# Row stages in wide steps, a last MLP chunk in an order of its own, and rows kept without the norm's weight and shift

## The chip, the cores and the metric

One core of a Trainium2 chip runs the whole program in one launch. The metric is the device time in microseconds (us); the kernel before has a median of 2984.6 us over 3 runs (2983.01 to 2986.8). Instructions run on five engines that wait for each other by semaphores: TensorE (PE, with its weight loads PEld), VectorE (DVE), ScalarE (ACT), GpSimd (POOL) and SyncE (SP), whose queue issues nearly all DMAs.

## The reference

Two transformer layers over 1024 image tokens and 256 context tokens of width 1024. Layer 0 mixes tokens by windowed attention with a sink beside a gated spatial mixing, layer 1 by neighbourhood attention on a 16 x 64 grid. What matters here is what stands around the mixers and in the MLP:

```python
def _layer_norm(x, g, b):
    mu = jnp.mean(xf, axis=-1, keepdims=True)
    var = jnp.mean(jnp.square(xf - mu), axis=-1, keepdims=True)
    y = (xf - mu) * lax.rsqrt(var + LN_EPS)
    return (y * g + b).astype(x.dtype)

def _squared_relu_mlp(h, w1, w2):
    return jnp.square(jax.nn.relu(h @ w1)) @ w2
```

In each layer the mixer reads h = x * (1 + scale_a) + shift_a and x becomes norm(ALPHA * x + gate_a * mixer(h)) with ln1's weight and shift; the MLP reads h = x * (1 + scale_m) + shift_m and x becomes norm(ALPHA * x + gate_m * mlp(h)) with ln2's. ALPHA is the square root of 2, and scales, shifts and gates are rows of 1024 numbers computed from the conditioning vectors, one set for the image tokens and one for the context tokens. Layer 1 gives image tokens only.

## The kernel before

Tokens lie in tiles of 128 rows: 10 in layer 0 (8 of the image, 2 of the context), 8 in layer 1. Every matrix product is done in three: both operands are split into a rounded high part and the low rest (`hth`/`htl` for the transposed activations, `wah`/`wal`, `wbh`/`wbl` for weights), and high x high, low x high and high x low are added in PSUM. The program is a row of eight stages with a barrier at the end of each:

- `stage_modulation` computes the first scales and shifts from 8 x 1 MB of weights; behind them SP fetches three tiles of x.
- `stage_rows(0, 0)`: each tile is transposed by TensorE (8 blocks of 128x128), modulated by ScalarE in 8 instructions of 128x128 (`modulate`, L388), then rounded and subtracted by VectorE (`split_ht`, L440 and L443) into `hth` and `htl`. The input has three buffers, so SP fetches tile t + 3 when tile t is transposed.
- `stage_window` (layer 0's attention, and the inputs of the mixing), and `stage_mix`: rows come from DRAM, are normalised (ScalarE L1287), mixed (PE L1349), completed (VectorE L1329, L1334), transposed, copied to `bot` (ScalarE L1293, `leave`; two buffers) and stored to `cat_dram` (SP L1279). SP issues the eight loads of the projection's weights `raww` (L1276) ahead of the first store.
- `stage_block(layer)`: first the projection, tile by tile: products, times the gate (L2147), plus ALPHA x (L2151, from `xres`, one buffer), moments, normalisation without weight and shift (L2163), transposes (L2267), modulation into `hth`. ln1's weight and shift are folded into the scale and shift columns (`fold`), so h is right without them; GpSimd applies them to the rows (L2057, L2059), and SP stores these in `x_dram` (L1912). ScalarE waits for the last store (`s_b`, `s_store`) before the MLP's first relu, because the MLP's buffers lie over those of the projection. In layer 1 the stored rows are fetched into `k.y` and multiplied by ALPHA (`begin_y`, L2111), and the MLP's sums are added there.
- The MLP runs in 16 chunks of 256 hidden columns. A step c does, for each group of 512 tokens, the second products of chunk c - 1 (`second`, L2305 to L2307) and then the first products of chunk c (L2329 to L2331), whose result passes ScalarE (relu L2032, square L2034), GpSimd (square in full precision L2078) and VectorE (the low part L2227). `sum_tile` (L2173) adds a tile's products into `y`. Steps are an instruction loop (`over_steps`); in layer 1 the last step is written out (`ending`), in layer 0 it is not: after the loop the second products of chunk 15 follow for all tiles, then per tile the gate (GpSimd L2085), ALPHA x and the moments (VectorE `residual`, L2180 to L2186), with x fetched into two buffers.
- `stage_rows(0, 2)`: between the layers: ln2 is applied by VectorE in two instructions a tile with rows of weight and shift (L475, L478), the result goes to `x_dram` and is transposed, modulated in 8 pieces, copied into grid order by ScalarE (`placed`, L395) and split by VectorE (L443).
- `stage_attention` (layer 1), and `stage_block(1)`, which ends in the output.

Every stage after the first clears the semaphores of the stage before; VectorE does it ahead of its first instruction (`clear_last`). Each engine carries out its instructions in the written order. `C` is 6, the number of VectorE counts a projection tile, and `nth(c, t)` numbers the second products.

## Time and profile before

| | |
|---|---|
| median of 3 runs | 2984.6 us (2983.01 to 2986.8) |
| profiled execution, its own time | 2985.59 us |
| its span | 2983.8 us, granted clock 0.967 |
| TensorE busy | 2799.8 us, 94% |
| VectorE busy | 1361.5 us, 46% |
| ScalarE busy | 912.1 us, 31% |
| GpSimd busy | 533.6 us, 18% |
| DMA | 238.95 MB, mean 80 GB/s |

The profile page cuts the span into 40 slices and gives each engine's busy share in tenths; the lines PEclk (granted TensorE clock) and DMA are on the same scale:

```profile
PE   6999995999999999999957999999799999999998
DVE  3575454563333333333383555555555333333336
PEclk7999997999999999999978999999999999999999
DMA  6574225441011010010042111110256111111112
```

A matmul's busy time overlaps the next one's, so a full PE slice tells that TensorE had work, not how fast it went. The dips of PE lie at the start, around slice 7 (460 to 510 us), around slices 21 and 22 (1500 to 1590) and around slice 29 (2150 to 2190).

### The profile page before, as it was taken

The page shows a single profiled execution, that of the slowest core. Times are in us where ns is not written, and L with a number is a line of the kernel's source. Part 1 is how long each engine was busy: PE and PEld are TensorE (multiplying, and loading weights), DVE is VectorE, ACT ScalarE, POOL GpSimd, SP SyncE. Part 2 cuts the span into 40 slices and gives each one's busy share as a digit, 9 for nine tenths or more (in the row PEclk, how much of TensorE's full clock was granted, in tenths as well). Part 3 has the DMA queues.
Part 4 walks back from the last instruction along what each step waited for, and adds up shares of the span by engine and source line. Part 5 has one row for each costly group of instructions (what it writes and reads, how often), then busy time and mean ns, then how long its engine had stood idle before and what let it go on. Part 6 is the DMA issues. An engine that isn't in the chain of part 4 may idle for free. (4 is left out here: it accounts for less than half of the span.)

```text
span 2983.8 us, 40578 instructions
## 1 busy us (share of the span) xinstructions
PE 2799.8 (94%) x15614; PEld 2296.1 (77%) x15614; DVE 1361.5 (46%) x2159; ACT 912.1 (31%) x1704; POOL 533.6 (18%) x365
## 2 busy tenths in 40 slices
PE   6999995999999999999957999999799999999998
PEld 3666774788888888888846888888677888888886
DVE  3575454563333333333383555555555333333336
ACT  4244553341121121111224344443433212211222
POOL 0000000341121121121140000000034223323321
PEclk7999997999999999999978999999999999999999
DMA  6574225441011010010042111110256111111112
GB/s 251 184 307 157 70 67 186 147 136 43 28 48 36 28 56 28 28 56 28 30 146 83 36 36 51 36 36 8 85 141 191 48 45 48 56 42 42 56 42 57
DMA packets 192673, 238.95 MB, mean 80 GB/s; under 512 B 15992, under 2 KB 153840, under 8 KB 186416
## 3 DMA queue, kind: packets, MB, share of 16 engines
q1 hardware_dynamic: 192272, 237.30, 24.8%
q8 instruction: 76, 1.25, 0.2%
q14 instruction: 37, 0.30, 0.0%
q10 hardware_dynamic: 288, 0.10, 0.0%
HBM read 203.72 MB, written 37.88 MB: 81 GB/s over the span
## 5 line engine op out<-in xcount | busy, mean ns | idle before, releaser
L2173 DVE TENSOR_TENSOR y<-y,pair 128x1024 f32<-128x1024 f32 x280 | 341.5, 1220 | 334.9 <-PE pair L2307 334.9
L2305 PE MATMUL pair<-m_wbh,m_ath 128*128 128x512 f32 x1120 | 437.1, 390 | 4.2 <-DVE y L2173 2.9
L2307 PE MATMUL pair<-m_wbh,m_atl 128*128 128x512 f32 x1120 | 437.9, 391 | 0.0
L2306 PE MATMUL pair<-m_wbl,m_ath 128*128 128x512 f32 x1120 | 436.9, 390 | 0.0
L2227 DVE TENSOR_TENSOR m_atl<-m_sq,m_ath 128x512 fp32r<-128x512 f32 x156 | 100.8, 648 | 646.2 <-POOL m_sq L2078 646.2
L2032 ACT ACTIVATE m_rel<-pair 128x512 f32<-128x512 f32 x160 | 88.9, 555 | 983.6 <-PE pair L2331 973.1
L2078 POOL TENSOR_TENSOR m_sq<-m_rel 128x512 f32<-128x512 f32 x160 | 155.2, 970 | 1125.6 <-ACT m_rel L2032 1125.5
L2331 PE MATMUL pair<-hth,m0n_wal 128*128 128x512 f32 (+1 forms) x768 | 272.2, 354 | 0.0
L2330 PE MATMUL pair<-htl,m0n_wah 128*128 128x512 f32 (+1 forms) x768 | 272.1, 354 | 0.0
L2329 PE MATMUL pair<-hth,m0n_wah 128*128 128x512 f32 (+1 forms) x768 | 271.5, 354 | 0.0
L2305 PEld LDWEIGHTS pair<-m_wbh,m_ath 128*128 128x128 f32 x1120 | 210.3, 188 | 50.3 <-DVE y L2173 4.6
L2307 PEld LDWEIGHTS pair<-m_wbh,m_atl 128*128 128x128 f32 x1120 | 210.2, 188 | 44.8
L2306 PEld LDWEIGHTS pair<-m_wbl,m_ath 128*128 128x128 f32 x1120 | 210.2, 188 | 44.5
L2329 PE MATMUL pair<-hth,m1n_wah 128*128 128x512 f32 x512 | 200.5, 392 | 3.4 <-DVE htl L2100 3.4
L2331 PE MATMUL pair<-hth,m1n_wal 128*128 128x512 f32 x512 | 200.8, 392 | 0.0
L2330 PE MATMUL pair<-htl,m1n_wah 128*128 128x512 f32 x512 | 200.7, 392 | 0.0
L2330 PEld LDWEIGHTS pair<-htl,m0n_wah 128*128 128x128 f32 x768 | 145.1, 189 | 21.6
L2329 PEld LDWEIGHTS pair<-hth,m0n_wah 128*128 128x128 f32 x768 | 145.1, 189 | 21.1
L2331 PEld LDWEIGHTS pair<-hth,m0n_wal 128*128 128x128 f32 x768 | 145.1, 189 | 20.1
L1611 DVE CUSTOM_DVE_ANT_0 a_sx<-pair,a_tab 128x640 f32<-128x640 f32 (+1 forms) x128 | 96.0, 787 | 86.8 <-PE pair L1703 86.8
L2025 ACT ACTIVATE m_wbh<-m_rawb 128x1024 fp32r<-128x1024 f32 x62 | 62.3, 1053 | 198.9 <-PE pair L2307 198.9
L2282 PE MATMUL pair<-r_wh,r_cath 128*128 128x512 f32 x288 | 116.5, 404 | 6.4 <-DVE r_catl L2095 5.9
(270 smaller groups left out, 5239.8 us busy)
## 6 DMA issues: line engine op xcount, KB each, us to landing
a_ring<-in_w_mod SPq DMA_DIRECT2D x40, 1024.0 KB, 9.1
m_rawb<-in_mlp_w SPq DMA_DIRECT2D x64, 512.0 KB, 4.4
m_rawa<-in_mlp_w SPq DMA_DIRECT2D x60, 512.0 KB, 4.1
x_rows<-r_res SPq DMA_DIRECT2D x28, 512.0 KB, 5.0
r_raw<-cat_cols SPq DMA_DIRECT2D x18, 512.0 KB, 6.3
mod_w<-in_w_mod SPq DMA_DIRECT2D x8, 1024.0 KB, 12.3
r_xin<-in_x SPq DMA_DIRECT2D x16, 512.0 KB, 4.3
gate_pre<-a0g_gout SPq DMA_DIRECT2D x20, 256.0 KB, 2.0
```

Of the source, the lines that this page charges most:

```text
L1611: dve.tensor_tensor_reduce(sx[:, n % 2, hh, 0:keys], two[:, at:at + keys], table(hh, t), -1.0, 3.0e38, ALU.add, ALU.min, sm[:, 0:1]).then_ ...
L2032: act.activation(rel[:, m % 2, 0:n], k.bank[4 + jj % NB1][:, 0:n], ACT.Relu).then_inc(s_relu, 1)
L2078: pool.tensor_tensor(sq[:, m % 2, 0:n], r, r, ALU.mult).then_inc(s_sq, 1)
L2173: dve.tensor_tensor(k.y[:, t, :], k.y[:, t, :], k.pair[t % 2][:, :], ALU.add).then_inc(s_y, 1)
L2227: dve.tensor_tensor(atl[:, m, a:a + n], sq[:, m % 2, 0:n], f32(ath[:, m, a:a + n]), ALU.subtract).then_inc(s_atl, 1)
L2282: pe.matmul(o, cath[:, t % 2, kt, :], wh[:, kt, n], start=kt == 0, stop=False)
L2305: pe.matmul(o, ath[:, m, ts], bh[:, m, cols], start=m == 0, stop=False)
L2306: pe.matmul(o, ath[:, m, ts], bl[:, m, cols], start=False, stop=False)
L2307: i = pe.matmul(o, atl[:, m, ts], bh[:, m, cols], start=False, stop=m == M - 1)
L2329: pe.matmul(o, wah[:, m, kt, :], xh, start=kt == 0, stop=False)
L2330: pe.matmul(o, wah[:, m, kt, :], xl, start=False, stop=False)
L2331: i = pe.matmul(o, wal[:, m, kt, :], xh, start=False, stop=kt == KT - 1)
```

## The change

All of these at once:

- **First rows stage** (`stage_first`): all ten tiles of x are fetched behind the modulation's weights. TensorE transposes four tiles before a group's first step is whole; a step is one block row of 128 features x 512 tokens (256 for the context). ScalarE modulates it in one instruction, and the rounding is VectorE's in even steps and ScalarE's in odd ones.
- **Mixing**: `bot` has six buffers, and each store is followed by one of the loads of `raww`.
- **Layer 0's last MLP chunk** has a step of its own, with the second products of chunk 15 begun before the first products end. x and the gate rows are fetched into the space of `hth`/`htl` (x in four buffers). GpSimd gates and VectorE adds and takes moments in an order written out by hand (`ending_first`).
- **Between the layers** (`stage_between`): wide steps as in the first stage. VectorE normalises in one instruction a tile, without weight and shift; ln2's are folded into layer 1's scale and shift columns; the eight image tiles are stored without them.
- **Layer 1's projection** reads these rows into two buffers, and GpSimd applies ln2's weight and shift to them before VectorE adds them. Its own rows are stored without ln1's weight and shift; `begin_y` applies these, in two instructions a tile where there was one. Only one gate row is fetched.
- **Clears** of semaphores are GpSimd's in each stage.

The core of the diff:

```diff
-            dve.sem_clear(s)
+            pool.sem_clear(s)
 # stage_modulation
-            for t in range(3):
-                sp.dma_start(x_ahead[:, t, :], io["x"][0][t * P:(t + 1) * P, :]).then_inc(s_ahead[t], 16)
+            for t in range(XT + CT):
+                sp.dma_start(x_ahead[:, t, :], x).then_inc(s_ahead[t], 16)
 # stage_first (stage_between alike, with placed() around hth and htl)
+            for i, (a, n, kt) in enumerate(steps):
+                act.wait_ge(s_tr, i + 1)
+                if i >= NB:
+                    act.wait_ge(s_hl, i - NB + 1)
+                act.activation(modt[:, i % NB, 0:n], k.bank[kt][:, 0:n], ACT.Identity, scale=col(SC_A), bias=col(SH_A)).then_inc(s_mod, 1)
+                if by_act(i):
+                    high(i)
...
+                if by_act(i):
+                    dve.wait_ge(s_ha, i // 2 + 1)
+                else:
+                    dve.tensor_copy(hi, v).then_inc(s_hd, 1)
+                    dve.wait_ge(s_hd, i // 2 + 1)
+                dve.tensor_tensor(k.htl[:, kt, a:a + n], v, f32(hi), ALU.subtract).then_inc(s_hl, 1)
 # stage_between, VectorE
+            def normalise(t):
+                dve.tensor_scalar(res[:, t, :], y[:, t, :], k.mv[:, t, 0:1], rstd[:, 1, t:t + 1], ALU.subtract, ALU.mult).then_inc(s_norm, 1)
 # stage_mix
-            for u in range(KT):
-                sp.dma_start(raww[:, u, :], io["ab_w_out"][0][u * P:(u + 1) * P, :]).then_inc(s_raww[u], 16)
+    NT = 6
+                if t < KT:
+                    sp.dma_start(raww[:, t, :], io["ab_w_out"][0][t * P:(t + 1) * P, :]).then_inc(s_raww[t], 16)
 # stage_block, layer 0, last chunk, TensorE
+                    if ends(c) and not final:
+                        if g == 0:
+                            second(c - 1, 1)
+                            second(c, 0)
+                        elif g == 1:
+                            second(c - 1, 2)
+                            second(c, 1, range(4, 7))
+                        else:
+                            second(c, 1, range(7, 8))
+                            second(c, 2)
 # the same, VectorE (ending_first)
+                for t in range(4):
+                    sum_tile(c, t)
+                    if t >= 2:
+                        residual(t - 2)
+                low(1, 0)
+                residual(2)
+                low(1, 1)
+                residual(3)
+                for t in range(8, tiles):
+                    sum_tile(c - 1, t)
+                for t in range(4, 7):
+                    sum_tile(c, t)
+                    if t == 6:
+                        residual(4)
+                for m in range(M):
+                    low(2, m)
+                residual(5)
+                for t in range(7, tiles):
+                    sum_tile(c, t)
+                    residual(t - 1)
+                residual(tiles - 1)
 # stage_block, layer 1, GpSimd
+            for t in range(tiles) if final else ():
+                pool.wait_ge(s_xr[t % 2], 16 * (t // 2 + 1))
+                x = xres[:, t % 2, :]
+                pool.tensor_tensor(x, x, lng[:, :], ALU.mult).then_inc(s_past, 1)
+                pool.wait_ge(s_past, 2 * t + 1)
+                pool.tensor_tensor(x, x, lnb[:, :], ALU.add).then_inc(s_past, 1)
 # begin_y, layer 1
-                        dve.tensor_scalar(k.y[:, t, :], k.y[:, t, :], ALPHA, None, ALU.mult).then_inc(s_y, 1)
+                        dve.scalar_tensor_tensor(out=y, in0=y, scalar=ALPHA, in1=ln1[0], op0=ALU.mult, op1=ALU.mult).then_inc(s_past, 1)
+                        dve.wait_ge(s_past, 2 * tiles + t + 1)
+                        dve.scalar_tensor_tensor(out=y, in0=ln1[1], scalar=ALPHA, in1=y, op0=ALU.mult, op1=ALU.add).then_inc(s_y, 1)
```

## Rows read from the trace of the kernel before

**Rows 1.** Windows by seam: start:end, length, busy us by engine, PEclk, DMA share, GB/s.
```profile
29.50:61.60 32.10, 18.05 (x80) 15.03 (x80) 19.18 (x20) 28.01 (x80) 0.00 (x0) 0.55 0.45 148
461.50:506.70 45.20, 21.73 (x129) 19.54 (x129) 17.87 (x37) 13.67 (x22) 0.00 (x0) 0.69 0.77 268
1492.30:1537.10 44.80, 28.55 (x120) 21.84 (x118) 38.57 (x51) 0.80 (x2) 31.83 (x11) 0.89 0.34 112
1537.10:1589.40 52.30, 19.68 (x80) 15.70 (x80) 37.91 (x39) 39.59 (x99) 0.00 (x0) 0.50 0.44 151
2147.50:2185.00 37.50, 27.68 (x102) 21.40 (x103) 18.55 (x23) 12.75 (x13) 0.00 (x0) 0.86 0.82 243
2262.00:2292.00 30.00, 23.78 (x95) 18.64 (x95) 18.59 (x19) 10.95 (x20) 15.19 (x8) 0.89 0.91 245
```

**Rows 2.** Timeline, first rows stage: start, us, instruction [idle before, releaser].
```profile
29.61 3.40 PE L530 MATMUL pair<-kept_ident,r_xin 128*128 128x128 f32 x16 [0.62 <-PEq L141]
...
34.52 0.69 DVE L440 CAST hth<-r_modt 128x1024 fp32r<-128x1024 f32 x1 [5.23 <-ACT r_modt L388]
```

**Rows 3.** Groups by line, first rows stage: busy us, mean ns, idle before.
```profile
L388 ACT ACTIVATE r_modt<-pair,kept_mod 128x128 f32<-128x128 f32 x80 | 28.0, 708 | 28.6 <-PE pair L530 28.6
```

**Rows 4.** DMA view of 0 to 62 us: GB/s in 40 slices.
```profile
GB/s 0 48 111 399 420 433 423 423 424 419 423 428 428 428 423 415 412 410 79 39 264 309 369 396 315 0 277 106 277 66 293 85 254 0 0 11 0 0 0 0
```

**Rows 5.** Page, costliest groups: busy us, mean ns, idle before.
```profile
L2227 DVE TENSOR_TENSOR m_atl<-m_sq,m_ath 128x512 fp32r<-128x512 f32 x156 | 100.8, 648 | 646.2 <-POOL m_sq L2078 646.2
```

**Rows 6.** Timeline of the mixing stage.
```profile
466.93 0.22 DVE L1308 RECIPROCAL gate_rstd<-gate_rstd 128x10 f32<-128x10 f32 x1 [10.87 <-issue]
...
472.52 0.76 DVE L1329 TENSOR_TENSOR gate_bo<-pair,gate_plus 128x256 f32<-128x256 f32 x2 [1.58 <-PE pair L1349]
...
489.64 0.60 ACT L1293 ACTIVATE gate_bot<-pair 128x512 f32<-128x512 f32 x1 [12.30 <-DMA cat_cols<-gate_bot]
```

**Rows 7.** Groups by line, 1495 to 1537 us, the end of layer 0's MLP.
```profile
L2183 DVE BATCH_NORM_STATS2 m_stats<-y 128x6 f32<-128x512 f32 x20 | 12.9, 685 | 0.3
L2180 DVE SCALAR_TENSOR_TENSOR y<-m_rawa,y 128x1024 f32<-128x1024 f32 x10 | 12.7, 1272 | 0.0
L2173 DVE TENSOR_TENSOR y<-y,pair 128x1024 f32<-128x1024 f32 x10 | 11.9, 1188 | 4.2 <-PE pair L2307 4.2
```

**Rows 8.** Timeline of GpSimd and TensorE there.
```profile
1496.43 2.40 POOL L2085 TENSOR_TENSOR y<-y,m_rawb 128x1024 f32<-128x1024 f32 x1 [3.06 <-DVE y L2173]
...
1501.81 3.32 POOL L2085 TENSOR_TENSOR y<-y,m_rawb 128x1024 f32<-128x1024 f32 x1 [0.30 <-DVE y L2173]
...
1509.36 0.50 PE L2305 MATMUL pair<-m_wbh,m_ath 128*128 128x512 f32 x1 [0.68 <-DVE y L2173]
```

**Rows 9.** Timeline, rows stage between the layers.
```profile
1543.43 0.21 DVE L454 RECIPROCAL r_rstd<-r_rstd 128x10 f32<-128x10 f32 x1 [6.54 <-DMA r_lnb<-in_ln_b]
...
1551.28 1.15 ACT L395 ACTIVATE hth<-r_modt 128x512 fp32r<-128x512 f32 x2
```

**Rows 10.** Instructions on the tile r_res: ns least/median/most, first and last start.
```profile
L2151 DVE SCALAR_TENSOR_TENSOR r_res<-r_xin,r_res x18: 1225/1904/2224, 533.5 to 2261.0; 128x1024 f32<-128x1024 f32 x18
L2163 DVE TENSOR_SCALAR r_res<-r_res,r_mv,r_rstd x18: 811/814/815, 536.9 to 2265.6; 128x1024 f32<-128x1024 f32 x18
```

**Rows 11.** Timeline, layer 1's projection and the MLP's first chunk.
```profile
2177.31 0.17 DVE L2125 COPY r_lnc<-pair 128x16 f32<-128x16 f32 x1 [10.14 <-DMA r_gate<-gate_rows]
...
2183.53 1.97 PE L2267 MATMUL pair<-kept_ident,r_res 128*128 128x128 f32 x8 [5.62 <-DVE r_res L2163]
...
2185.68 2.39 POOL L2057 TENSOR_TENSOR r_res<-r_res,r_lng 128x1024 f32<-128x1024 f32 x1 [88.51 <-PE pair L2267]
...
2276.49 0.79 PE L2329 MATMUL pair<-hth,m1n_wah 128*128 128x512 f32 x1 [3.43 <-DVE htl L2100]
...
2277.68 0.60 ACT L2032 ACTIVATE m_rel<-pair 128x512 f32<-128x512 f32 x1 [6.07 <-DMA x_rows<-r_res]
...
2291.49 0.49 PE L2305 MATMUL pair<-m_wbh,m_ath 128*128 128x512 f32 x1 [1.24 <-DVE y L2111]
```

657 lines of the change are left out of this document (281 added, 376 removed).

## The prediction

> **What bounds the kernel now.** I first cut the span by stages (busy time in windows). In the matmul stages TensorE is busy for all but a few per cent of the window and its granted clock is near 1.00; what is slower is six seams, and the change touches all of them: the first rows stage, the mixing stage, the end of layer 0's MLP, the rows stage between the layers, and the two ends of layer 1's projection [rows 1]. In these TensorE is busy for 18 of 32, 22 of 45, 29 of 45, 20 of 52, 28 of 38 and 24 of 30 us. So I read the timeline of each engine in those windows alone and asked there which wait ends last. The matmuls of the long stretches keep their number and shapes, so I give them no change.
>
> **First rows stage, 32.1 us now.** ScalarE sets it: 80 modulations of 128x128 take 28.0 us, 0.35 each [rows 3]. They become 24, sixteen of 128x512 and eight of 128x256, plus 12 rounding copies that alternate with VectorE. A 128x512 read of PSUM costs ScalarE 0.60 [rows 6], a 128x512 copy 0.58 (half of 1.15) [rows 9]; instructions that follow each other without a wait overlap by about 0.1. A pair of wide steps is 0.50 + 0.60 + 0.55 = 1.65, eight pairs 13.2; the four pairs of half size at 1.1 are 4.4. ScalarE's sum is 17.6. VectorE has per pair one cast (0.69 for 1024 columns, so about 0.4 for 512 [rows 2]) and two subtractions of 0.65 [rows 5]: 1.7, the same speed. What is new is the wait ahead of it: the first step needs the 25th of 32 transposes (0.21 each, from 16 in 3.40 [rows 2]), so it starts at 29.6 + 5.3 = 34.9, not at 31.6. The loads cover that: 8.4 MB of weights and then tiles of 0.52 MB stream at some 420 GB/s (each figure of the row is 1.55 us of the window) [rows 4], so tiles 0 to 2, in already, are followed by tile 3 at about 29.5 and tile 9 at 37. End: 34.9 + 17.6 + 1.5 for the last chain and the barrier = 54.0 at best; VectorE and ScalarE wait for each other through four buffers, so I take 55, against 61.6: **-6.5** (ends -9, if the loads and the overlap are perfect, and 0).
>
> **Mixing stage, 45.2 us now.** Two waits. VectorE starts at 466.93, having cleared the old semaphores since 461.6; without them it starts when the square root is done, some 3.5 earlier [rows 6]. Second, ScalarE's third copy out waits 12.30 for a store that is queued behind the eight loads of the projection's weights (4.2 MB) [rows 6]. With six output buffers and one load per store this wait goes. What is late next: the products begin at about 470 instead of 472.5 [rows 6], and a pair of tiles costs VectorE 2.9 (0.76 for two halves and 0.69, twice) plus the turn through TensorE and ScalarE, 3.5 to 4.5, so the fifth pair is out by 488 to 491. Then the queue: the 5.2 MB of gate rows end at about 477, and 4.2 MB of weights and 2.6 MB of stores remain; at 400 GB/s they need 17 us, that is until 494.5, and the last store is behind them. End 495, against 506.7: **-11.5** (-15 if arithmetic sets the end, -7 at the stage's mean of 268 GB/s [rows 1], which would give 500 to 502). The next stage starts no earlier by the clears alone: its first low part waits for the load of the columns anyway. Nothing there.
>
> **End of layer 0's MLP, 44.8 us now.** After the last first product, ten tiles pass through VectorE one by one (sum 1.19, residual 1.27, two moments of 0.69, aggregate 0.2: about 3.8 a tile), and TensorE waits some 0.7 for it in each [rows 7, 8]; TensorE alone needs 2.73 for the twelve products of a tile (3.8 less the wait and less the slower start after it). The change moves the products of four tiles ahead of the second first-product and three ahead of the third. I laid VectorE's written order against TensorE's, counting from P, the start of the last chunk's first four tiles (1470.2 now, 22.15 before 1492.3). GpSimd's gating takes 2.4 alone, 3.3 when VectorE runs beside it [rows 8]; I use 3.3. Gating of tiles 0 to 3 ends P+17.1 and holds the square of the second group by 0.1 only. Tile 8 of the chunk before is summed at P+28.1, and TensorE, ready at 27.6, waits 0.5. TensorE ends at P+50.2. VectorE is late: sum of tile 8 at 51.3, residual 7 at 54.0, sum 9 at 55.2, its gating at 58.5, last residual P+61.2 = 1531.4 against 1536.9: **-5.5** (-9 with gating at 2.4 and no slip, 0 if VectorE's two extra waits for squares, at most 2.7 each, each fall late).
>
> **Rows stage between, 52.3 us now.** VectorE first waits 6.54, for clears and the norm's rows [rows 9]; then ten tiles in 46 us, in lockstep with ScalarE's eight small modulations. After: square root and reciprocal until +0.65; two normalisations at 0.81 [rows 10], four small folds of 0.2, two more normalisations: the fourth tile is ready at +4.6, its transpose and the first wide modulation at +5.5. From there VectorE: eight pairs of a cast and two subtractions, 0.45 + 0.65 + 0.65 and 0.1 of gaps (14.8), four half pairs of 1.1 (4.4), six normalisations in between (4.7): 23.9. ScalarE has 18.5 beside it and is covered. End +29.4, with the barrier 30, against 52.3: **-22** (-25 to -18). The cast writes runs of eight columns; no row has it, so I bound it by half the contiguous one, 0.35, and the subtraction's 0.65; eight of them move the sum by 2.4 at most, and I take 0.45. The Trainium skill bears on this (VectorE: DVE Perf Modes, What auto-detection actually checks): a single-source operation inside SBUF takes the double rate where the outermost dimensions are equal, which it would here; that puts the cast near the low end. The trace agrees for the contiguous one, 0.69 for 1024 columns [rows 2]; no row shows the strided. By the rule the sum would be 0.8 better, by the other end 1.6 worse.
>
> **Layer 1's projection, this one costs.** First end. VectorE now begins when the second gate row lands, 2177.3, and the residual row lands at 2179.3; tile 0 is normalised and TensorE's transposes, 5.62 late, run at 2183.53 [rows 11]. One gate row fewer puts the first residual row in its place, 2177.3. But GpSimd must then multiply and add on it: 2 x 2.4 and gaps, 4.9 [rows 11], so VectorE gets it at 2182.2, 2.9 later than now, and beside GpSimd on the second tile its 1.22 becomes 1.9 (least and median) [rows 10]: **+3.6** (0 to +5). In the middle the row's path is load 5 + GpSimd 4.9 + VectorE 1.9 = 12, and with two buffers it has the time of two tiles. From tile 0's transposes at 2183.5 to the wait at 2276.5 [rows 11] eight tiles pass, over 11 each, so 22: covered.
> Other end. The last row's weight and shift, 4.8 on GpSimd ahead of the last store, go. ScalarE's first relu waits for that store now [rows 11]. So the relu moves from 2277.7 to 2275, the last low part of h from 2276.5 to 2274.9 (TensorE waits 3.43 for it now [rows 11]), and the last five rows of y are fetched 5 earlier. But y then needs two operations of 1.22 a tile where one of 0.69 did, and TensorE's first product on y waits for seven tiles, its second for all eight. VectorE is free for tiles 1 to 7 at about 2281; 7 x 2.5 = 17.5, so 2295.9 for the seventh, against 2291.49 now [rows 11]: +4.5. TensorE then stands for some 7 us instead of 1.24. After the stall of 3.43 its two jobs took 13.8 instead of 10.9, so a restart at a low clock costs 2 to 3; one moves from 2276 to 2296. I count nothing more for it. Other end **+4.5** (0 to +9). Both are ahead of a stretch in which TensorE is never short of work, so nothing gives them back.
>
> **Clears on GpSimd** elsewhere: in the window and attention stages TensorE's first matmuls wait for its own ten warm-up matmuls, and GpSimd's tables are wanted tens of us later. Nothing. Instructions of the last chunk, now written out once more, run as in layer 1: nothing.
>
> **Sum.** -6.5 - 11.5 - 5.5 - 22 + 3.6 + 4.5 = -37.4. The profiled execution took 2985.6 (span 2983.8 and 1.8 around it); it lies 1.0 above the median of 2984.6, so 2947 to 2948. I say 2948. The own range of this case is 2938 to 2957.
>
> **Rivals.**
> 1. The seams are bound by something else soon. For it: in the mixing stage a queue of 6.8 MB, in the MLP's end VectorE's written order, where one late square shifts all behind it; in layer 1, two stands and two cold restarts. Against: each length above is a sum of rows. With the weak ends, 0, -7, 0, -18, +5, +9: -11, with half of these slips -24: 2962, band 2957 to 2978. Chance 0.20.
> 2. Layer 1's additions are hidden: the residual row lands so early that GpSimd is done when the gate is, and y is ready in time, since loads come 5 earlier. For it: VectorE is idle through much of that stretch. Against: its order puts y behind the low parts of the chunk. The sum without them: 2940, and with better ends in the other seams 2932. Chance 0.13.
> 3. Slower: TensorE's clock. The last chunk of layer 0 now has a hand-over between VectorE and TensorE at each of some 20 products, and the clock could fall in them. A restart costs 2.9 (13.8 against 10.9, above); from 14 of them the gains are gone, and with 16 it is 2994. Against: now TensorE stops 0.7 at each of ten tiles in the MLP's end, and only the first product after a stop is longer, 0.50 [rows 8]. Chance 0.03.
> 4. The parts don't add: GpSimd's clears stand in the way of its work on the first rows, or something unseen. Near 2982, chance 0.02.
>
> **How the numbers follow.** The forecast has 0.62. The range takes in rival 2's middle and rival 1's nearer half: 2936 to 2962. A difference of 0.2% is 6 us, about what can be told from none: under 2979 is faster. That holds for the forecast, rival 2 and nearly all of rival 1: 0.95; same 0.02, slower 0.03.
>
> **What would show it.** First rows stage: 24 modulations and an end near 55. Mixing: no idle over 2 us ahead of the copy out, and a stage of some 34. MLP's end: VectorE's last residual about 11 after TensorE's last product. Between: 30 long, VectorE nearly full. Layer 1: GpSimd's two operations between the landing and the first residual, and seven y tiles in a row ahead of the first product on y. I am wrong if the between stage is over 35, or if the delay on y is absent.

## The result, and the profile after

| | before | after |
|---|---|---|
| median, runs of the same session | 2985.7 us (4 runs, 2983.01 to 2987.27) | 2969.0 us (4 runs, 2967.44 to 2971.22) |
| ratio | | 0.9946 (95% interval 0.9928 to 0.9963) |
| profiled execution, its own time | 2985.6 us | 2971.2 us |
| its span, granted clock | 2983.8 us, 0.967 | 2969.4 us, 0.973 |

The kernel is faster by 16.7 us, and 37 were forecast: the sign is right, the size is not, and 2969.0 lies outside the range of 2936 to 2962. The windows of the seams show where, start:end in us, length, busy us by engine, then PEclk, DMA share and GB/s. They answer to those of before [rows 1] in the same order; the third starts with the last chunk and not with its end, and the last two are a little longer than their counterparts.

```profile
30.02:56.62 26.60, 14.41 (x80) 11.06 (x79) 18.23 (x36) 21.18 (x37) 0.04 (x1) 0.76 0.44 149
...
455.00:492.31 37.31, 19.79 (x129) 17.73 (x130) 18.12 (x37) 13.61 (x23) 0.00 (x0) 0.73 0.92 325
...
1456.00:1519.80 63.80, 50.49 (x241) 41.34 (x239) 45.94 (x57) 4.08 (x8) 31.41 (x14) 0.96 0.19 56
1519.80:1551.05 31.25, 14.90 (x81) 13.38 (x82) 25.73 (x51) 21.69 (x38) 0.04 (x1) 0.72 0.52 186
...
2109.70:2152.00 42.30, 27.04 (x96) 20.28 (x96) 19.52 (x23) 12.66 (x13) 10.18 (x4) 0.78 0.68 209
...
2230.00:2300.00 70.00, 49.01 (x199) 38.83 (x198) 45.45 (x35) 15.08 (x26) 23.72 (x12) 0.85 0.55 158
```

To compare kernels I cut every trace at the same instructions: TensorE's first warm-up matmul behind each rows stage and at the start of layer 1's projection, VectorE's last copy of layer 0's attention, ScalarE's first copy of the projection's weights, the end of VectorE's last aggregate of layer 0 (`moments`), TensorE's transposes of layer 1's first tile. Lengths in us:

| stretch | before | after | change | forecast |
|---|---|---|---|---|
| start to the end of the first rows stage | 61.9 | 56.6 | -5.3 | -6.5 |
| layer 0's window attention | 393.7 | 394.0 | +0.3 | 0 |
| mixing | 51.1 | 41.7 | -9.4 | -11.5 |
| layer 0's projection and MLP | 1030.2 | 1027.5 | -2.7 | -5.5 |
| between the layers | 52.6 | 31.3 | -21.3 | -22 |
| layer 1's attention | 558.1 | 558.7 | +0.6 | 0 |
| layer 1's projection, up to the first transposes | 35.9 | 42.2 | +6.3 | +3.6 |
| from there to the end | 800.3 | 817.4 | +17.1 | +4.5 |
| span | 2983.8 | 2969.4 | -14.4 | -37.4 |

Layer 0 gave 38.5 of the 45.5 forecast. The loss is in layer 1: 24.1 where 8.1 were priced, and 12.6 of the difference lies in the last stretch. Its timeline there (start in us, duration in us, instruction, and in brackets the idle time before it and what ended it), first VectorE:

```profile
2252.79 2.07 DVE L2039 SCALAR_TENSOR_TENSOR y<-y,r_over 128x1024 f32<-128x1024 f32 x1
2254.89 1.22 DVE L2041 SCALAR_TENSOR_TENSOR y<-r_over,y 128x1024 f32<-128x1024 f32 x1
...
2266.45 3.37 DVE L2039 SCALAR_TENSOR_TENSOR y<-y,r_over 128x1024 f32<-128x1024 f32 x1
2269.85 3.25 DVE L2041 SCALAR_TENSOR_TENSOR y<-r_over,y 128x1024 f32<-128x1024 f32 x1
2273.02 3.39 DVE L2039 SCALAR_TENSOR_TENSOR y<-y,r_over 128x1024 f32<-128x1024 f32 x1
2276.44 3.28 DVE L2041 SCALAR_TENSOR_TENSOR y<-r_over,y 128x1024 f32<-128x1024 f32 x1
```

GpSimd's in the same us, the low parts of the first weight and the gating of the second:

```profile
2265.69 6.33 POOL L1987 TENSOR_TENSOR m1n_wal<-m_rawa,m1n_wah 128x1024 fp32r<-128x1024 f32 x2 [6.28 <-ACT m1n_wah L1923]
2271.98 6.66 POOL L1993 TENSOR_TENSOR m_rawb<-m_rawb,y 128x1024 f32<-128x1024 f32 x2
```

And what TensorE and ScalarE do about it:

```profile
2273.33 0.79 PE L2273 MATMUL pair<-m_wbh,m_ath 128*128 128x512 f32 x1 [15.88 <-DVE y L2041]
2273.91 0.63 PE L2274 MATMUL pair<-m_wbl,m_ath 128*128 128x512 f32 x1
```
```profile
2246.53 0.60 ACT L1947 ACTIVATE m_rel<-pair 128x512 f32<-128x512 f32 x1 [6.56 <-DMA x_rows<-r_res]
```

The seven tiles of y were priced at 7 x 2.5 = 17.5. They take from 2252.79 to 2279.7, 26.9, and the last four operations take 3.25 to 3.39 each, not 1.22. That is not a slower VectorE: GpSimd's pairs of operations take 6.33 and 6.66 in those us. In layer 0 such a pair, beside VectorE's sums of y, leaves both engines at their own times:

```profile
1095.54 4.76 POOL L1987 TENSOR_TENSOR m0n_wal<-m_rawa,m0n_wah 128x1024 fp32r<-128x1024 f32 x2 [0.87 <-ACT m0n_wah L1923]
```
```profile
1096.36 1.22 DVE L2106 TENSOR_TENSOR y<-y,pair 128x1024 f32<-128x1024 f32 x1 [1.23 <-PE pair L2275]
```

The difference is where the inputs lie: those of the sum are `y` and `pair`, which is in PSUM, while both inputs of the operations that begin y are in SBUF. With both there, each engine stands while the other runs. (By the Trainium skill, SBUF — State Buffer, "SBUF: two separate sides", the port pair that GpSimd and VectorE share is "an exclusive lock, not a bandwidth split", and a VectorE operation with two SBUF inputs takes it against a GpSimd operation that reads SBUF; these rows agree.)

TensorE has finished the first products by 2257.4 and stands 15.88. The relu, forecast 2.7 earlier than its old place, is where it was: the kernel is 31.5 ahead at the transposes (2183.53 against 2151.99), and 2246.53 + 31.5 is 2278.1, against 2277.68 [rows 11]. The last store still lands only at 2246.4. It is issued at 2234.82 and takes 11.6 us to land; in the kernel before it was issued at 2272.63 and landed at 2277.50, after 4.9.

The first end of the projection, VectorE and then GpSimd:

```profile
2138.68 0.17 DVE L2055 COPY r_lnc<-pair 128x16 f32<-128x16 f32 x1 [8.39 <-DMA r_gate<-gate_rows]
...
2145.72 3.27 DVE L2084 SCALAR_TENSOR_TENSOR r_res<-r_xin,r_res 128x1024 f32<-128x1024 f32 x1 [5.16 <-POOL r_xin L1974]
```
```profile
2140.86 2.34 POOL L1972 TENSOR_TENSOR r_xin<-r_xin,r_lng 128x1024 f32<-128x1024 f32 x1 [81.54 <-DMA r_xin<-x_rows]
2143.28 2.34 POOL L1974 TENSOR_TENSOR r_xin<-r_xin,r_lnb 128x1024 f32<-128x1024 f32 x1
2145.58 2.34 POOL L1972 TENSOR_TENSOR r_xin<-r_xin,r_lng 128x1024 f32<-128x1024 f32 x1
```

VectorE's addition is released at 2145.72, 0.14 behind the start of GpSimd's multiplication of the second tile, and lasts 3.27: until that one is done (2147.92), and then 1.07, nearly its own 1.2.

### The profile page after: what moved, and what is told of

It reads as the page before. It is cut to its first block and busy times, and to the rows that moved or that the text cites. A ratio compares the mean times of both kernels' runs of the same rounds, so it can differ in the third digit from the quotient of the medians.

```text
span 2969.4 us, 40552 instructions
## 1 busy us (share of the span) xinstructions
PE 2793.5 (94%) x15615; PEld 2289.2 (77%) x15615; DVE 1367.4 (46%) x2195; ACT 887.6 (30%) x1598; POOL 533.5 (18%) x365
## 3 DMA queue, kind: packets, MB, share of 16 engines
q8 instruction: 78, 1.28, 0.2%
## 5 line engine op out<-in xcount | busy, mean ns | idle before, releaser
L2273 PE MATMUL pair<-m_wbh,m_ath 128*128 128x512 f32 x1080 | 422.1, 391 | 16.8 <-DVE y L2041 16.8
L2275 PE MATMUL pair<-m_wbh,m_atl 128*128 128x512 f32 x1080 | 423.2, 392 | 0.0
L2274 PE MATMUL pair<-m_wbl,m_ath 128*128 128x512 f32 x1080 | 422.2, 391 | 0.0
L2273 PEld LDWEIGHTS pair<-m_wbh,m_ath 128*128 128x128 f32 x1080 | 203.4, 188 | 60.7 <-issue 16.3
L2275 PEld LDWEIGHTS pair<-m_wbh,m_atl 128*128 128x128 f32 x1080 | 203.3, 188 | 43.3
L2274 PEld LDWEIGHTS pair<-m_wbl,m_ath 128*128 128x128 f32 x1080 | 203.3, 188 | 43.2
L2296 PEld LDWEIGHTS pair<-htl,m0n_wah 128*128 128x128 f32 x768 | 145.1, 189 | 21.6
## 6 DMA issues: line engine op xcount, KB each, us to landing
mod_w<-in_w_mod SPq DMA_DIRECT2D x8, 1024.0 KB, 12.2
```

Of the source, the lines that this page charges most:

```text
L2273: pe.matmul(o, ath[:, m, ts], bh[:, m, cols], start=m == 0, stop=False)
L2274: pe.matmul(o, ath[:, m, ts], bl[:, m, cols], start=False, stop=False)
L2275: i = pe.matmul(o, atl[:, m, ts], bh[:, m, cols], start=False, stop=m == M - 1)
L2296: pe.matmul(o, wah[:, m, kt, :], xl, start=False, stop=False)
```

## The experiments

Differences of a whole run are given against the changed kernel's 2969.0, from medians; each ratio is to the kernel before, measured on the same chip, whose median moved between 2984.3 and 2986.2 from one chip or session to the next. Differences of 2 us in the whole are therefore not told from none, and there I read the stretches above. They come from the profiled execution, and the changed kernel's took 2971.2, 2.2 above its median: a stretch can show up to 2 us more than the medians do. The diffs are cut to the lines that matter; the semaphores that go with them are left out.

**1. GpSimd waits for y.**

```diff
+                if final and not starts(c):
+                    pool.wait_ge(s_y, tiles)
```

> GpSimd's weight work for the second chunk (the low part of w1, the gate on w2) waits until all eight y tiles are begun. Theory A (VectorE's two-input operations on y and GpSimd's two-input operations block each other): the four y operations that took 3.3 to 3.4 us fall to 1.2, y is complete some 8 us earlier after the relu, and the whole is 7 to 9 us faster than the changed kernel (near 2961). Theory B (the y operations are slow because the fetches of w1 and w2 run then): they stay at 3.3, no change. Theory C (GpSimd's work is itself due at that time): TensorE waits for the low part of w1 instead, and what is gained is given back, within 2 us of the changed kernel.

Measured: 2964.9 us, ratio 0.9929 (0.9913 to 0.9946), 4.1 less; the last stretch is 811.5, 5.9 less. Groups by line over 2100 to 2340 us (busy us, mean ns, idle before):

```profile
L2041 DVE SCALAR_TENSOR_TENSOR y<-y,r_over 128x1024 f32<-128x1024 f32 x8 | 12.1, 1512 | 5.0 <-DMA y<-x_rows 5.0
...
L2043 DVE SCALAR_TENSOR_TENSOR y<-r_over,y 128x1024 f32<-128x1024 f32 x8 | 9.8, 1225 | 0.3
```

The second operation is back at 1.225 us in all eight tiles (a mean of 1.734 in the changed kernel), though the fetches of the weights run on: theory B is out. Tiles 1 to 7 take 18.5 us and not 26.9. TensorE's waits for y fall only from 16.8 to 12.2, because its first product on y waits for the sixth of these seven tiles, 3.8 us earlier in the stretch than in the changed kernel, and the seventh is then done before it is wanted. So the blocking is real. What this run takes away of it is worth 5.9 in the last stretch, less than half of what the end lost; two first operations of 2.06 and 2.07 beside GpSimd's squares stay. The whole gains less than theory A's 7 to 9 and more than theory C's 2, and what C names isn't seen: up to 2340 us TensorE waits for nothing of GpSimd's.

**2. One operation for y.**

```diff
-                        dve.scalar_tensor_tensor(out=y, in0=y, scalar=ALPHA, in1=ln1[0], op0=ALU.mult, op1=ALU.mult).then_inc(s_past, 1)
...
-                        dve.scalar_tensor_tensor(out=y, in0=ln1[1], scalar=ALPHA, in1=y, op0=ALU.mult, op1=ALU.add).then_inc(s_y, 1)
+                        dve.tensor_scalar(y, y, ALPHA, None, ALU.mult).then_inc(s_y, 1)
```

> begin_y in layer 1 is one multiplication by ALPHA again; ln1's weight and shift are left out of the residual. Theory A (the second operation and the block with GpSimd are the price of this seam): the first second product comes within 1 us of where the kernel before has it, counted from the end of the projection, so 15 to 17 us faster than the changed kernel (near 2953). Theory B (the store of the last rows sets it, as it did before): the gain is at most 3 us.

Measured: 2955.4 us, ratio 0.9896 (0.9879 to 0.9912), 13.6 less. TensorE's and VectorE's groups over 2100 to 2300 us:

```profile
L2271 PE MATMUL pair<-m_wbh,m_ath 128*128 128x512 f32 x32 | 13.2, 412 | 3.8 <-DVE y L2039 3.8
```
```profile
L2039 DVE TENSOR_SCALAR y<-y 128x1024 f32<-128x1024 f32 x8 | 5.7, 747 | 9.8 <-DMA y<-x_rows 9.8
```

TensorE's wait is 3.8 and no longer 16.8, and the last stretch is 802.6: 14.8 of its 17.1 are back. The medians show a little less than theory A's 15 to 17, and theory B's 3 is out. What this end lost is, but for 2.3 us, y's two operations with what blocks them; this run takes out both at once and doesn't divide them.

**3. Residual rows without GpSimd.**

```diff
-                pool.tensor_tensor(x, x, lng[:, :], ALU.mult).then_inc(s_past, 1)
...
-                pool.tensor_tensor(x, x, lnb[:, :], ALU.add).then_inc(s_past, 1)
```

> GpSimd's multiplication and addition on layer 1's residual rows are left out (ln2's weight and shift are missing in that residual). Theory A (GpSimd's two operations stand in front of tile 0's residual, and with it its next one blocks VectorE): tile 0's residual starts when its row has landed, and transposes of tile 0 come 6 to 7 us earlier, all of which is kept: near 2962.5. Theory B (the row's landing sets it): at most 2 us.

Measured: 2964.0 us, ratio 0.9928 (0.9911 to 0.9944), 5.1 less; the stretch up to the first transposes is 7.6 shorter, and those begin at 2143.87:

```profile
2139.65 1.23 DVE L2080 SCALAR_TENSOR_TENSOR r_res<-r_xin,r_res 128x1024 f32<-128x1024 f32 x1 [0.29 <-DMA r_xin<-x_rows]
```

The row is then ready when the gate is, and the addition takes 1.23. GpSimd's two operations cost 7.6 here, which is theory A; the spans of the profiled executions differ by 7.6 as well, the medians by 5.1. The last stretch is as long as in the changed kernel (817.9 against 817.4): the two ends are separate.

**4. Clears on VectorE.**

```diff
-            k.clear_last(pool)
+            k.clear_last(dve)
```

> Only the clearing of the old semaphores goes back from GpSimd to VectorE, in every stage. Theory A (a clear costs about 0.1 us and counts where VectorE is first in line): mixing stage 2 to 3.5 us longer, rows stage between 5 to 6.5 longer, nothing in the other stages: 7 to 10 us slower than the changed kernel (near 2977.5). Theory B (clears are hidden by loads and tables): under 2 us.

Measured: 2976.0 us, ratio 0.9965 (0.9952 to 0.9977), 7.0 more. The two places where VectorE cleared, in the mixing and between the layers:

```profile
460.00 0.22 DVE L1059 RECIPROCAL gate_rstd<-gate_rstd 128x10 f32<-128x10 f32 x1 [10.85 <-issue]
```
```profile
1524.85 0.22 DVE L1190 RECIPROCAL r_rstd<-r_rstd 128x10 f32<-128x10 f32 x1 [6.95 <-issue]
```

Between the layers the wait is 6.95 where the changed kernel has 0.64, and block and clears together are 6.8 longer. In the mixing VectorE starts 3.7 later (10.85 behind its last copy, 7.15 in the changed kernel), and the stage is 41.2 us against 41.7: no longer at all. So theory A holds between the layers and fails in the mixing, where the clears were worth nothing, and the total of 7.0 is all from the one place.

**5. The last store ahead of y.**

```diff
-                    for i in range(2):
-                        sp.wait_ge(s_store[i], 16 * len(range(i, 3, 2)))
-                    for u in range(3):
-                        sp.dma_start(k.y[:, u, :], rows(k.x_dram, u, True)).then_inc(s_yx[u], 16)
                 for u in ([t - 1] if 0 < t < tiles - 1 else [t - 1, t] if t else []):
...
+                for i in range(2):
+                    sp.wait_ge(s_store[i], 16 * len(range(i, 3, 2)))
+                for u in range(3):
+                    sp.dma_start(k.y[:, u, :], rows(k.x_dram, u, True)).then_inc(s_yx[u], 16)
```

> SP fetches the first three rows of y behind the last stores of layer 1's projection, no longer ahead of them; nothing else is changed. Theory A (the last store, issued at 2234.12 and landed at 2246.4, waits in the queue behind loads that nothing ahead of the MLP's second step needs): the first relu of layer 1's MLP starts some 3 to 6 us earlier than its 2246.5, but VectorE's rows of y, which set the end, start no earlier than the low parts of h allow, so the time falls by 1 to 5: 2964 to 2968. Rival B (the store is slow by itself, or bound by the loads of the weights ahead of it): the relu moves by under 1.5 and the time stays at 2969 within 2. Rival C (y's first row lands later and VectorE then waits for it): slower, 2970 to 2974.

Measured: 2973.0 us, ratio 0.9959 (0.9945 to 0.9973), 4.0 more (3.2 in the last stretch): rival C. The store is indeed faster: issued at 2232.51, it lands at 2239.19, after 6.7 us and not 11.6. Groups of TensorE and of ScalarE over 2100 to 2310 us:

```profile
L2295 PE MATMUL pair<-hth,m1n_wah 128*128 128x512 f32 x48 | 19.8, 412 | 6.0 <-DVE htl L2025 6.0
```
```profile
L1947 ACT ACTIVATE m_rel<-pair 128x512 f32<-128x512 f32 x6 | 3.6, 595 | 50.0 <-PE pair L2297 42.5 <-DVE htl L2025 7.4
```

The relu no longer waits for the store but for the last low part of h, and this for y's first row, which lands at 2241.42 and which VectorE's order puts ahead of it. TensorE waits 6.0 for the low part (3.3 in the changed kernel). Two late waits lie side by side; mending one shows the other.

**6. The gate row behind the first residual row.**

```diff
+            if final:
+                residual_in(0)
             for c in range(3 - XB):
-                sp.dma_start(rgate[:, c, :], gate_row).then_inc(s_row, 16)
-            for t in range(XB):
+                sp.dma_start(rgate[:, c, :], gate_row).then_inc(s_rg if final else s_row, 16)
+            for t in range(1 if final else 0, XB):
                 residual_in(t)
...
-            pool.wait_ge(s_row, 48 if final else 64)
+            pool.wait_ge(s_row, 32 if final else 64)
```

> At layer 1's first end the loads go in the order weight row, shift row, residual row 0, gate row, residual row 1, and GpSimd waits only for the first three. Theory A (tile 0 is late because GpSimd's multiplication and addition start only when the gate row has landed): GpSimd starts some 2 us earlier, TensorE's transposes of tile 0 are 2 to 3 earlier (2149 to 2150 instead of 2152), and the time is 2966 to 2968. Rival B (VectorE's addition, 3.27 while GpSimd works on the second tile, and not the loads, is what is late): GpSimd starts earlier but VectorE, which waits for the gate, meets GpSimd at another place; the transposes move by under 1 and the time is 2969 within 1.5.

(In the diff the DMA's address is shortened to `gate_row`.) Measured: 2965.9 us, ratio 0.9937 (0.9921 to 0.9954), 3.1 less; the transposes come 2.3 earlier in their stretch, and GpSimd starts at 2135.99, 2.4 earlier in it: theory A. VectorE's timeline:

```profile
2138.46 0.17 DVE L2062 TENSOR_TENSOR kept_mod<-kept_mod,r_lnt 128x16 f32<-128x16 f32 x1
2138.55 2.32 DVE L2063 TENSOR_TENSOR kept_mod<-kept_mod,r_lnc 128x16 f32<-128x16 f32 x1
2140.79 1.28 DVE L2082 TENSOR_TENSOR r_res<-pair,r_gate 128x512 f32<-128x512 f32 x2
2142.10 2.12 DVE L2089 SCALAR_TENSOR_TENSOR r_res<-r_xin,r_res 128x1024 f32<-128x1024 f32 x1
```

An operation of 16 columns takes 2.32 instead of 0.17, because GpSimd began 2.38 us of work at 2138.46. In this the blocking is seen at its barest: its price is what is left of the other engine's instruction, whatever the size of one's own. Rival B is thus seen too, but it takes back only 0.1 of the 2.4.

**7. Mixing: three weight loads ahead of the first store.**

```diff
+            for u in range(3):
+                sp.dma_start(raww[:, u, :], io["ab_w_out"][0][u * P:(u + 1) * P, :]).then_inc(s_raww[u], 16)
...
-                if t < KT:
+                if t + 3 < KT:
```

> In the mixing stage three of the eight loads of the projection's weights are issued ahead of the first store, the other five behind stores 0 to 4, instead of eight behind eight stores. Theory A (the stage ends 7 us after its last store is issued because that store queues behind 4.2 MB of loads issued just before it): the loads get done earlier while the queue is slack, the stage ends 2 to 4 us earlier than its 492.3, and the time is 2965 to 2967. Rival B (the queue is full from the stage's start, by the gate rows of 5.2 MB, so order doesn't matter): stage and time stay within 1.5 of 492.3 and 2969. Rival C (ScalarE waits for stores again): the copies out wait over 3 us and the time is over 2970.

Measured: 2971.1 us, ratio 0.9953 (0.9937 to 0.9970), 2.1 more; the stage is 41.8 us (41.7 in the changed kernel). That is rival B's stage, and theory A is out; the time lies 0.6 above B's bound, which the differences between sessions cover. ScalarE does wait for stores again, as rival C has it, but for 1.53, 1.28 and 1.40 us and not over 3, and the stage doesn't show it. The mixing of the changed kernel, 450 to 493 us in 40 slices:

```profile
GB/s 0 204 71 40 44 8 0 192 345 250 345 341 373 356 398 410 406 391 381 387 373 400 392 389 374 415 367 408 372 393 394 389 399 380 402 379 333 101 14 0
```

From about 458.6 to 490 us the queue carries 333 to 415 GB/s, but for one slice (each is 1.08 us), 12.5 MB in the whole window. From the stage's first issue at 456.57 on, the stage is the time of its transfers: weights loaded earlier or an earlier start of VectorE (experiment 4) don't shorten it. Two things stay untried: weights loaded behind the last store, and transfers in the 6 us before that first issue, in which the queue is nearly idle (0 to 71 GB/s from the third slice on).

**8. y interleaved with the sums.**

```diff
+        if final:
+            body(1)
...
                         for t in tiles_of(g):
                             sum_tile(c - 1, t)
+                            if final and isinstance(c, int) and c == 1 and g == 0:
+                                begin_y(t + 4, t + 5)
...
-                            begin_y(1, tiles)
+                            begin_y(1, 4)
```

> Layer 1's y: VectorE begins only tiles 0 to 3 ahead of the second step, and tiles 4 to 7 one by one between the sums of tiles 0 to 3, so TensorE's first product on y waits for three tiles' operations and not for seven. The same operations, the same sum of work. Theory A (the lost 12 us of this end are a wait of TensorE for seven tiles in a row, of which 9.4 are GpSimd's and VectorE's blocking of each other): TensorE's idle time ahead of its first product on y falls from 16.8 to 5 to 8 us, later waits of 1 to 2 come in its place, and the time is 2957 to 2962. Rival B (VectorE has no slack in the second step, so what is moved comes back as waits between the products): the time is over 2965. Rival C (GpSimd's two low parts of the weights, delayed by VectorE, take the place of the wait): TensorE's wait stays above 12 and the time is over 2964.

Measured: 2952.8 us, ratio 0.9889 (0.9873 to 0.9906), 16.2 less, more than theory A gave. TensorE's groups over 2100 to 2310 us:

```profile
L2307 PE MATMUL pair<-hth,m1n_wah 128*128 128x512 f32 x64 | 26.3, 412 | 4.4 <-DVE htl L2029 4.4
L2285 PE MATMUL pair<-m_wbh,m_ath 128*128 128x512 f32 x41 | 16.2, 395 | 0.7 <-DVE y L2116 0.7
```

The wait of 16.8 is 0.7, and B and C are out. The last stretch is 801.0, and it was 800.3 before the change. The work is the same and the blocking is still there, as the next rows show, but it costs TensorE nothing, because four of the tiles are wanted later:

```profile
2268.30 2.29 DVE L2043 SCALAR_TENSOR_TENSOR y<-y,r_over 128x1024 f32<-128x1024 f32 x1
2270.63 3.31 DVE L2048 SCALAR_TENSOR_TENSOR y<-r_over,y 128x1024 f32<-128x1024 f32 x1
```

**9. The same, and y's tile 0 behind the last low part of h** (the diff is against experiment 8).

```diff
-            begin_y(0, 1 if final else XT)
             split_ht(tiles - 1)
+            if final:
+                begin_y(0, 1)
```

> The interleaved y of the run before, and VectorE begins y's tile 0 behind the last low part of h, no longer ahead of it. Theory A (the last low part waits for y's first row to land, and TensorE for the low part): TensorE's wait at the last first-product of tile 7, 4.4 us in the interleaved run and 3.3 in the changed kernel, falls under 1, its next first-products run at the high clock, and the time falls by 2 to 6 against 2952.8: 2947 to 2951. Rival B (the relu, which waits for the last store until 2247, holds the squares and so TensorE's second products): TensorE's wait only moves to the second products, the time stays within 1.5 of 2952.8. Rival C (VectorE is at the low parts too early and blocks with GpSimd's rows of the second weight): over 2954.

Measured: 2953.3 us, ratio 0.9898 (0.9881 to 0.9914), 0.5 from experiment 8: rival B. TensorE's groups over 2100 to 2340 us:

```profile
L2310 PE MATMUL pair<-hth,m1n_wah 128*128 128x512 f32 x87 | 34.1, 391 | 1.2 <-DVE htl L2029 1.2
L2288 PE MATMUL pair<-m_wbh,m_ath 128*128 128x512 f32 x64 | 26.1, 408 | 5.3 <-DVE y L2119 4.4 <-DVE m_wbl L2171 0.8
```

The wait for the low part falls from 4.4 to 1.2, and 4.6 more come back at the second products, most of it as a wait for VectorE's first sum, which stands behind its row of y.

**10. Gating of 64 columns in layer 0's last chunk.**

```diff
-                pool.tensor_tensor(y, y, end_gate[cond(t)], ALU.mult).then_inc(s_gated, 1)
+                pool.tensor_tensor(k.y[:, t, 0:64], k.y[:, t, 0:64], end_gate[cond(t)][:, 0, 0:64], ALU.mult).then_inc(s_gated, 1)
```

> GpSimd's gating in layer 0's last chunk covers 64 of 1024 columns (the rest of the gate is left out). Theory A (the end of layer 0's MLP is 2.6 later than laid out since GpSimd's 2.4 to 3.3 us a tile stand in VectorE's way, 2.2 of it in one sum): the last sum and residual fall by 4 to 5, that is the wait for the last gating and the blocked operation, and the time is 2964 to 2966. Rival B (VectorE's own written order sets the end and GpSimd is covered): the stage moves by under 1.5 and the time stays at 2969 within 2. Rival C (TensorE's products come late because of waits for squares): no move, and TensorE shows more than its 0.8 of waits.

Measured: 2968.7 us, ratio 0.9945 (0.9928 to 0.9962), 0.3 less: neither theory A's 3 to 5 nor, by its stage, rival B. All low parts of the last chunk, duration in ns least/median/most, first of the changed kernel, then of this one:

```profile
L2170 DVE TENSOR_TENSOR m_atl<-m_sq,m_ath x6: 426/692/2587, 1441.6 to 1499.7; 128x512 fp32r<-128x512 f32 x4, 128x256 fp32r<-128x256 f32 x2
```
```profile
L2170 DVE TENSOR_TENSOR m_atl<-m_sq,m_ath x6: 425/692/693, 1441.6 to 1499.7; 128x512 fp32r<-128x512 f32 x4, 128x256 fp32r<-128x256 f32 x2
```

VectorE's part of theory A is seen: the operation of 2.59 is 0.53 (GpSimd's gating at 1499.57 had held it), and the block ends 2.2 earlier. The total doesn't show it. The next stage is 1.2 longer: its first 32 transposes take 6.59 instead of 5.20, at a granted clock of 0.56 instead of 0.71, for which I have no cause. 1.4 more are lost in layer 1, in code that is the same. Whether the 2.2 can be had stays open.

**11. All of 5, 6, 8 and 9** (each line of the diff with its place as a comment).

```diff
+                residual_in(0)            # ahead of the gate row
+                begin_y(t + 4, t + 5)     # behind the sum of tile t
+                begin_y(0, 1)             # behind split_ht(tiles - 1)
+                sp.dma_start(k.y[:, u, :], rows(k.x_dram, u, True)).then_inc(s_yx[u], 16)  # behind the last stores
```

> The changed kernel with y interleaved, y's tile 0 behind the last low part, the first three rows of y fetched behind the last stores, and the gate row fetched behind the first residual row. Theory A (what is lost in layer 1 is the sum of these): against the changed kernel 3 from the gate row, 16 from the interleaving and 3 to 6 from the last low part and the earlier store: 2943 to 2948, and so at or under the forecast of 2948. Rival B (the parts share one wait, that of the relu for the store): not under 2949. Rival C (y's first rows, fetched behind the stores, are then late for VectorE): TensorE waits over 3 us ahead of its first product on y, and the time is 2950 or more.

Measured: 2953.3 us, ratio 0.9892 (0.9876 to 0.9909). Theory A's 2943 to 2948 is missed. The numbers fit rival B and rival C: the relu is early (2241.59), but VectorE then waits 2.35 for y's first row, and TensorE 4.33 for VectorE's first sum. Layer 1's two stretches are 3.6 shorter than in experiment 8 (598.8 and 799.8, from the end of the between stage on, against 601.2 and 801.0), but in this profile layer 0's block took 1.6 and the mixing 1.0 longer, in code that is the same.

**12. Only 6 and 8.**

```diff
+                residual_in(0)            # ahead of the gate row
+                begin_y(t + 4, t + 5)     # behind the sum of tile t
```

> The changed kernel with two of the mends alone: y interleaved with the sums, and the gate row fetched behind the first residual row. Theory A (the two waits lie at different ends of the projection and have nothing in common): 16 and 3 less than the changed kernel's 2969, 2949 to 2951. Rival B (in the run with all mends together the gate row's 2.4 us came out at TensorE's transposes and were given back later): 2952 to 2954, as in that run.

Measured: 2950.9 us, ratio 0.9884 (0.9867 to 0.9900), 18.1 less than the changed kernel and the fastest of all: theory A. The total alone wouldn't tell it from experiment 8 or 11. The stretches are 598.6 and 799.8, the same as with all four mends. So the moves of the stores and of y's tile 0 bring nothing on top of these two. In 11 the mixing and layer 0's block were 3.1 longer together than here (42.4 and 1030.4 against 41.4 and 1028.3); I have no cause for that.

## Why the prediction was wrong

**The step that failed** is "y then needs two operations of 1.22 a tile ... 7 x 2.5 = 17.5 ... +4.5". It was right that TensorE would wait for a row of y's tiles, and the prediction named the wait. The size was wrong, +17.1 (the figures in the old time are those of the changed kernel plus 31.5):
- The length of the row of operations: 26.9 for seven tiles, not 17.5, and 20.3 for the first six, not 15. The working priced VectorE's operations as if GpSimd stood still. The rows for it were there: the same kind of operation at 1.9 and 2.2 beside GpSimd [rows 10], used for the other end and not for this one. Experiments 1 and 10 show the blocking as such.
- Its start: 2252.79 + 31.5 = 2284.3 in the old time, and 2281 was forecast, since the relu didn't move. "The last row's weight and shift, 4.8 on GpSimd ahead of the last store, go" held, and the store was issued 6.3 earlier than before; but it now stood behind the loads issued just ahead of it and landed after 11.6 us and not 4.9. Experiment 5 shows that an earlier store isn't even enough: the low part of h waits for y's first row beside it.
- The first product on y is thus late by 4.4 (forecast) + 5.3 + 3.3 = 13.0; measured 13.4 (2273.33 - 2151.99, against 2291.49 - 2183.53 [rows 11]). The other 3.7 pass before the second product, which waits for the eighth tile, 4.1 later still than laid out. The restart, which I had counted as moved at no cost, didn't move: TensorE still waits 3.3 for the low part, and starts slowly once more at y, where the first products take 0.79 and 0.63 and settle at 0.39 (granted clock 0.55 from 2273.0 to 2279.7, 1.00 behind it). It lies in the same us as the wait for the eighth tile.

Experiment 2 bears this out: with y's one operation as before, 14.8 come back in this stretch, this term's miss of 12.6 and 2.2 of its 4.5.

**First end, +3.6 forecast, +6.3 measured, right in kind.** The chain is as told (gate, GpSimd, VectorE), but the last link was priced by the median of 1.9 and took 3.27, with GpSimd's multiplication of the second tile in its way; 7.6 was the whole cost of GpSimd's two operations (experiment 3). The residual row was there at 2140.86, 31.2 behind the stage's start of 2109.7; before, it was there 31.8 behind it (2179.3). One gate row fewer gained 0.6, not 2. -0.6, 4.9 for GpSimd and 2.0 for the longer addition are the 6.3.

**Mixing, -11.5, -9.4.** "Then the queue" was the right binding term: the queue is full from 2 us behind the stage's first issue on, so the 12.5 MB set it. By the slices the transfers end at about 490.5, that is 495.5 in the old time of this stage (5.0 more), where 494.5 was worked out. The rest of the miss lies between there and ScalarE's first copy at 492.31, 1.8 us where 0.5 was laid out for the last store. The earlier start of VectorE, put at 3.5, did not enter that sum, and is worth nothing (experiment 4).

**End of layer 0's MLP, -5.5, -2.7.** The written order came out within 2.6 of the working: VectorE's last at P + 63.8 for P + 61.2, with P at 1455.98. One low part of 256 columns, released 0.08 behind the start of a gating, took 2.59 for 0.43: 2.2 of the 2.6.

```profile
1499.57 2.38 POOL L2009 TENSOR_TENSOR y<-y,m_over 128x1024 f32<-128x1024 f32 x1
```
```profile
1499.65 2.59 DVE L2170 TENSOR_TENSOR m_atl<-m_sq,m_ath 128x256 fp32r<-128x256 f32 x1 [2.45 <-POOL m_sq L2000]
```

**First rows stage and between, -6.5 and -22, measured -5.3 and -21.3: right within 1.2.** The groups of the between stage, beside 80 modulations of before [rows 3] and its first reciprocal [rows 9]:

```profile
L1187 ACT ACTIVATE r_modt<-pair,kept_mod 128x512 f32<-128x512 f32 (+1 forms) x24 | 15.6, 695 | 8.1 <-PE pair L1240 8.0
...
L1222 DVE TENSOR_TENSOR htl<-r_modt,hth 128x512 fp32r<-128x512 f32 (+1 forms) x24 | 14.3, 601 | 1.1 <-ACT hth L1190 0.7
...
L1220 DVE CAST hth<-r_modt 128x512 fp32r<-128x512 f32 (+1 forms) x12 | 4.5, 378 | 3.4 <-ACT r_modt L1187 3.4
```

A pair of wide steps goes by every 2.00 us, where 1.65 (ScalarE) and 1.85 (VectorE) were worked out. The term that was too small is ScalarE's: two wide modulations take 1.43 and not 1.10, since their price was that of another operation on PSUM. In the first rows stage ScalarE goes without a stop from 34.23 to 55.78, 21.6 for the 17.6 of the sum; an earlier start, a shorter end and the 1.0 of slack take up all but 1.2. Between the layers VectorE has ten normalisations beside its steps and is nearly full either way: its waits in the rows above are 1.1 and 3.4, of which 2.64 at the start. The strided cast took 0.42 for the 0.45 laid out.

**The signs.** Those that the prediction named were nearly all seen: 24 modulations, no stop over 2.1 us ahead of the copy out, VectorE's last residual 10.6 behind TensorE's last product, a between stage of 31, and the delay on y. They told that each mechanism was there, and not how long it was.

**The rivals.** Rival 1, "bound by something else soon", is the nearest: 2969 lies in its band of 2957 to 2978, and the queue, VectorE's order in the MLP's end and two stands in layer 1 are what it names. But the blocking, which made the two ends of layer 1 long, is in none of its parts. Rival 2's condition, that the additions are hidden, is false as written; experiments 8 and 12 show that it can be made true for y, while at the first end 4.0 stay (39.9 against 35.9). Rival 3 (clock in the last chunk) is out: granted clock 0.96 there. So is rival 4, since the parts of the table add up. All the misses had one sign. The three ends with GpSimd beside VectorE were missed by pricing each engine's operations alone; the mixing and the first rows stage were not.

## What to carry to other kernels

Work moved from one engine to another costs its time on the engine that receives it, and what it blocks on the engine it shares a port with; so where VectorE's operations with two inputs in SBUF meet GpSimd's, add the two engines' times. Before adding operations ahead of a consumer, ask how many of their results the consumer's first instruction needs, and write only those ahead of it: the same work in another order was worth 16 of the 17 us. And a store that an engine waits for stands behind the loads issued before it; but look at the wait next to it before moving it, since here an earlier store alone made the kernel slower (experiment 5).

## What the runs showed of the hardware

- A VectorE operation with two inputs in SBUF that starts behind a GpSimd operation lasts until that one's end and then its own time, less some 0.15: 3.27 for 1.23 (1024 columns), 2.59 for 0.43 (256), 2.32 for 0.17 (16).
- With one of the two inputs in PSUM there is no such wait: the changed kernel's sums `y<-y,pair` take 1.22 each, those that start while GpSimd works as well. Nor are VectorE's moments longer there, which read y alone: 0.68 to 0.70. But a single input is no safe sign: in the kernel before, the multiplication of y by ALPHA that starts at 2271.10, beside GpSimd, takes 2.06 for 0.69.
- A cast that writes runs of eight columns (`hth` between the layers) takes 0.42 us for 512 columns, as the contiguous one of the first rows stage does; the mean of 0.378 has four of 256 columns at 0.29 in it.
- The transfers of the mixing, reads and writes in one queue, hold 333 to 415 GB/s over 31 us, but for one slice of 250.
- Stretches with the same code differ between profiles: layer 0's window attention took 390.9 to 394.0 in the thirteen variants, and the between stage, from VectorE's first reciprocal on, 30.5 to 31.8. A gain of 2 us in one seam is seen in that seam and not in the total.
